# Expert rows of a two-layer decoder step: gated and added by VectorE from loaded rows, or scaled at PSUM eviction and added by accumulating transfers

## The reference, cut to what matters

```
prob  = softmax(x @ router_w)                     # choose a group of 4, then its best 2 experts
gate  = prob[two experts] / sum(prob[two experts])
out   = sum over the two: gate * ((silu(x @ w_gate) * (x @ w_up)) @ w_down[e])
x     = layer_norm(ALPHA * x + out) * g + b       # ALPHA = 4 ** 0.25, eps = 1e-5
```

## Time and profile before

| | |
|---|---|
| median of 3 runs | 1471.41 us (1467.73 to 1471.97) |
| profiled execution, from first to last instruction | 1465.0 us |
| TensorE busy | 1253.8 us, 86% |
| VectorE busy | 916.1 us, 63% |
| ScalarE busy | 698.6 us, 48% |
| GpSimd busy | 252.7 us, 17% |

### The profile page before, as it was taken

One profiled execution on the slowest core, in us unless ns is written; L12 is line 12 of the kernel. 1 busy time (PEld: TensorE's weight loads), 2 busy tenths in 40 slices (PEclk: granted clock), 3 DMA queues, 4 the chain that ended last, 5 costly groups with the idle time before them and its releaser, 6 DMA issues.

```text
span 1465.0 us, 16900 instructions
## 1 busy us (share of the span) xinstructions
PE 1253.8 (86%) x5888; PEld 963.9 (66%) x5888; DVE 916.1 (63%) x1112; ACT 698.6 (48%) x748; POOL 252.7 (17%) x261
## 2 busy tenths in 40 slices
PE   5989994599999996299999999989937999999930
PEld 4766764478888885277776666657736788888820
DVE  4256357498888885832321444464675988888836
ACT  4233223277777775222112544432224777777721
POOL 2021020241111121410000000000302411112314
PEclk9999995699999998599999999969858999999975
DMA  9302047269999996732230133213462899999842
GB/s 341 122 29 93 1 173 285 84 224 359 374 372 372 376 368 214 296 116 92 89 116 1 59 116 115 78 48 118 187 238 83 302 376 373 369 375 371 299 181 77
DMA packets 142529, 302.56 MB, mean 207 GB/s; under 512 B 11888, under 2 KB 12048, under 8 KB 142352
## 3 DMA queue, kind: packets, MB, share of 16 engines
q1 hardware_dynamic: 123024, 250.23, 47.9%
q0 software_dynamic: 19168, 51.31, 9.8%
q10 hardware_dynamic: 288, 0.36, 0.1%
HBM read 288.36 MB, written 30.28 MB: 217 GB/s over the span
## 4 chain that ended last, share of the span: by engine, by line
PE 78%; DVE 13%; DMA 3%; ACT 3%; issue 2%; POOLq 0%; POOL 0%; SPq 0%; DVEq 0%; ACTq 0%
PE ps L1422 20%; PE ps L1424 20%; PE ps L1423 20%; PE ps L1657 3%; DVE wl L868 2%; PE ps L1720 2%; PE ps L1705 2%; PE ps L1581 2%; DVE x L1225 2%; PE ps L1467 2%; ACT wh L617 2%; PE ps L1674 1%; PE ps L1691 1%; DMA xg<-x_rows,gcur 1%; DMA yl<-y_rows 1%
## 5 line engine op out<-in xcount | busy, mean ns | idle before, releaser
L868 DVE TENSOR_TENSOR wl<-raw,wh 128x2048 fp32r<-128x2048 f32 x210 | 481.0, 2314 | 221.3 <-ACT wh L617 217.4
L617 ACT ACTIVATE wh<-raw 128x2048 fp32r<-128x2048 f32 x210 | 398.4, 1915 | 202.0 <-PE ps L1424 138.0
L1422 PE MATMUL ps<-wh,xTh 128*128 128x512 f32 (+1 forms) x560 | 227.7, 407 | 22.8 <-DVE wl L868 14.8
L1424 PE MATMUL ps<-wh,xTl 128*128 128x512 f32 (+1 forms) x560 | 223.0, 398 | 0.0
L1423 PE MATMUL ps<-wl,xTh 128*128 128x512 f32 (+1 forms) x560 | 223.0, 398 | 0.0
L1422 PE MATMUL ps<-wh,xgTh 128*128 128x512 f32 x512 | 209.3, 409 | 6.7 <-DVE xgTl L1175 5.7
L1423 PE MATMUL ps<-wl,xgTh 128*128 128x512 f32 x512 | 203.9, 398 | 0.0
L1424 PE MATMUL ps<-wh,xgTl 128*128 128x512 f32 x512 | 203.5, 398 | 0.0
L1422 PEld LDWEIGHTS ps<-wh,xTh 128*128 128x128 f32 (+1 forms) x560 | 98.6, 176 | 58.9 <-issue 22.5
L1422 PEld LDWEIGHTS ps<-wh,xgTh 128*128 128x128 f32 x512 | 97.3, 190 | 36.2 <-DVE wl L868 8.3
L1424 PEld LDWEIGHTS ps<-wh,xTl 128*128 128x128 f32 (+1 forms) x560 | 98.0, 175 | 34.2
(11 more groups left out here) (258 smaller groups left out, 1641.1 us busy)
## 6 DMA issues: line engine op xcount, KB each, us to landing
raw<-in_moe_w_up SPq DMA_DIRECT2D x120, 1024.0 KB, 10.5
raw<-in_moe_w_down SPq DMA_DIRECT2D x62, 1024.0 KB, 11.7
raw<-in_a_w_in SPq DMA_DIRECT2D x8, 1024.0 KB, 16.7
ahead_up<-in_moe_w_up SPq DMA_DIRECT2D x8, 1024.0 KB, 8.7
yl<-y_rows POOLq DMA_DIRECT2D x8, 1024.0 KB, 8.4
raw<-in_cache_k SPq DMA_DIRECT2D x16, 512.0 KB, 3.8
raw<-in_cache_v SPq DMA_DIRECT2D x16, 512.0 KB, 4.9
raw<-in_a_w_out SPq DMA_DIRECT2D x4, 1024.0 KB, 5.1
```

The lines of the kernel that those rows point to most:

```text
L617: act.activation(wh[:, slot], src, ACT.Copy).then_inc(high[key], 1)
L868: dve.tensor_tensor(wl[:, slot], src, wh[:, slot].bitcast(F32), ALU.subtract).then_inc(low[key], 1)
L1422: pe.matmul(out, high_, w_high, start=start, stop=False)
L1424: return pe.matmul(out, low_, w_high, start=False, stop=stop)
```

## The change

`y_out_` now evicts with a scale for each row: `gslot[:, i]`, the gate of the token in that row divided by ALPHA. `gslot` is built like the index lists: VectorE makes `hi32` (block one-hots times gate / ALPHA), ScalarE widens `lo16` to `lo32`, TensorE multiplies them in ten float32 matmuls, VectorE copies the result from PSUM (`gate_columns`). The rows of `y_rows` are so already gated. Ten accumulating transfers add them to x in SBUF: five with the first choices, then five with the second, each of which GpSimd issues after the first one on the same tile has landed. The sum is x + out / ALPHA instead of ALPHA * x + out; the layer norm divides that factor out again, with eps / ALPHA^2. The multiplies by ALPHA on GpSimd, the buffer `yl` and VectorE's two multiply-adds for each tile are gone. Some semaphores are merged, which moves nothing.

```diff
@@ SyncE
-                    sp.wait_ge(y_in[4], 16)
+                    sp.wait_ge(y_in[4], 32)
@@ GpSimd, moe_pool
-                scale(range(0, 2))
                 gather(3)
-                scale(range(2, 3))
                 scatter(0)
-                scale(range(3, TILES))
...
-                pairs = y_rows[l].rearrange("(k n) d -> n k d", k=2)
-                for t in range(TILES):
-                    pool.dma_start(yl[0:ROWS[t], t], dram_tile(t, pairs)).then_inc(y_in[t], 16)
+                for k in range(2):
+                    for t in range(TILES):
+                        if k:
+                            pool.wait_ge(y_in[t], 32 * l + 16)
+                        pool.dma_start(x[0:ROWS[t], t], dram_tile(t, y_rows[l][k * NTOK:(k + 1) * NTOK]),
+                                       accum_op=ALU.add).then_inc(y_in[t], 16)
                 gain(2 + 2 * l, x)
@@ ScalarE, y_out_ and before the first xg_high
-                    act.activation(yb[:], ps[:, 4:6].rearrange("p a n -> p (a n)"), ACT.Copy).then_inc(s["y_ready"], 1)
+                    act.wait_ge(gate_list, l + 1)
+                    act.activation(yb[:], ps[:, 4:6].rearrange("p a n -> p (a n)"), ACT.Copy,
+                                   scale=gslot[:, bass.ds(i, 1)]).then_inc(s["y_ready"], 1)
...
+                act.wait_ge(onehots, l + 1)
+                act.activation(lo32[:], lo16[:], ACT.Copy).then_inc(slots32, 1)
@@ VectorE, end of route, before xg_low(0), add_experts
-                link(dve.tensor_tensor(gates[:], gates[:], col[:, 6, 1].unsqueeze(1).broadcast_to([P, 2, TILES]),
-                                       ALU.mult))
+                link(dve.scalar_tensor_tensor(out=gates[:], in0=gates[:], scalar=1.0 / ALPHA,
+                                              in1=col[:, 6, 1].unsqueeze(1).broadcast_to([P, 2, TILES]),
+                                              op0=ALU.mult, op1=ALU.mult))
+                link(dve.tensor_tensor(hi32[:], iota[:, 0:LIST_COLS].unsqueeze(1).broadcast_to(hi_shape),
+                                       block_of.broadcast_to(hi_shape), ALU.is_equal))
+                dve.tensor_tensor(hi32[:], hi32[:],
+                                  gates[:].rearrange("p k t -> p (k t)").unsqueeze(2).broadcast_to(hi_shape), ALU.mult
+                                  ).then_inc(gates_at, 1)
...
+            def gate_columns(l):
+                dve.wait_ge(gate_sums, l + 1)
+                dve.tensor_copy(gslot[:], ps[:, 7, 0:LIST_COLS]).then_inc(gate_list, 1)
...
                 def produce(t):
-                    m = ROWS[t]
-                    dve.wait_ge(s["scaled"], t + 1)
-                    dve.wait_ge(y_in[t], 16 * (l + 1))
-                    for k in range(2):
-                        link(dve.scalar_tensor_tensor(out=x[0:m, t], in0=yl[0:m, t, k], scalar=gates[0:m, k, t:t + 1],
-                                                      in1=x[0:m, t], op0=ALU.mult, op1=ALU.add))
+                    dve.wait_ge(y_in[t], 32 * (l + 1))
@@ TensorE, before turn_x(0)
+                pe.wait_ge(slots32, l + 1)
+                pe.wait_ge(gates_at, l + 1)
+                for n in range(2 * TILES):
+                    mm = pe.matmul(ps[:, 7, 0:LIST_COLS], lo32[:, n], hi32[:, n], start=(n == 0),
+                                   stop=(n == 2 * TILES - 1))
+                mm.then_inc(gate_sums, 1)
                 turn_x(0)
```

More of the change, by code:

```diff
@@ L214, in trunk @@
         hb, n = place("hb", [P, HALF], F32, n)
+        lo32, _ = place("lo32", [P, 2 * TILES, P], F32, n)
         hTh, n = place("hTh", [P, 4, P], F32R, n)
@@ L217, in trunk @@
         yb, n = place("yb", [P, D], F32, n)
-        yl, _ = place("yl", [P, TILES, 2, D], F32, arena)
         lg, n = place("lg", [P, TILES, EXPERTS], F32, n)
@@ L234, in trunk @@
         hi16, n = place("hi16", [P, 2 * TILES, LIST_COLS + 1], F16, n)
+        hi32, n = place("hi32", [P, 2 * TILES, LIST_COLS], F32, n)
+        gslot, n = place("gslot", [P, LIST_COLS], F32, n)
         ahead_up = [place(f"ahead_up{q}", [P, 4, HALF], F32, xT_at + q * slot_bytes)[0] for q in range(4)]
@@ L249, in trunk @@
         pages_in = sem("pages_in")
-        x0_high = sem("x0_high"); x0_low = sem("x0_low")
-        rw_high = sem("rw_high"); rw_low = sem("rw_low")
+        inputs_high = sem("inputs_high"); inputs_low = sem("inputs_low")
         wsm_zeroed = sem("wsm_zeroed"); ws_masked = sem("ws_masked")
@@ L282, in trunk @@
         logit_max = sem("logit_max"); plan = sem("plan"); onehots = sem("onehots"); masks = sem("masks")
+        slots32 = sem("slots32"); gates_at = sem("gates_at"); gate_sums = sem("gate_sums"); gate_list = sem("gate_list")
         moe = [{k: sem(f"{k}{l}") for k in (
             "gcopy", "gathered", "xg_tr", "xg_high", "xg_low", "silu", "h_ready", "h_tr", "h_high", "h_low",
-            "y_ready", "scopy", "scattered", "xg_zero", "scaled")} for l in range(LAYERS)]
+            "y_ready", "scopy", "scattered", "xg_zero")} for l in range(LAYERS)]
         ident = con[:, C_IDENT:C_IDENT + P]
@@ L528, in scatter @@
                                             bounds_check=2 * NTOK - 1, oob_is_err=False).then_inc(s["scattered"], 16)
-                def scale(tiles):
-                    for t in tiles:
-                        m = ROWS[t]
-                        pool.tensor_scalar(x[0:m, t], x[0:m, t], ALPHA, None, ALU.mult).then_inc(s["scaled"], 1)
                 gather(0)
@@ L660, in _ @@
                 act.wait_ge(xT0_in[half], 32)
-                act.activation(xTh[:, 4 * half:4 * half + 4], xT0[:, 4 * half:4 * half + 4], ACT.Copy).then_inc(x0_high, 1)
+                act.activation(xTh[:, 4 * half:4 * half + 4], xT0[:, 4 * half:4 * half + 4], ACT.Copy).then_inc(inputs_high, 1)
                 split_a(half)
             act.wait_ge(rw_in, 16)
-            act.activation(rwh, rw_raw[:], ACT.Copy).then_inc(rw_high, 1)
+            act.activation(rwh, rw_raw[:], ACT.Copy).then_inc(inputs_high, 1)
             for j in range(4):
@@ L891, in ln_stats @@
                 link(dve.bn_aggr(mv[0:m, t], stats[0:m, t].rearrange("p a b -> p (a b)")))
-                dve.tensor_scalar(lns[0:m, 0, t:t + 1], mv[0:m, t, 1:2], EPS, None, ALU.add).then_inc(ln_var, 1)
+                eps = EPS / ALPHA ** 2 if call in (2, 4) else EPS
+                dve.tensor_scalar(lns[0:m, 0, t:t + 1], mv[0:m, t, 1:2], eps, None, ALU.add).then_inc(ln_var, 1)
             def ln_scale(call, t):
@@ L942, in _ @@
             for half in range(2):
-                dve.wait_ge(x0_high, half + 1)
+                dve.wait_ge(inputs_high, half + 1)
                 w = (slice(None), slice(4 * half, 4 * half + 4))
-                dve.tensor_tensor(xTl[w], xT0[w], xTh[w].bitcast(F32), ALU.subtract).then_inc(x0_low, 1)
+                dve.tensor_tensor(xTl[w], xT0[w], xTh[w].bitcast(F32), ALU.subtract).then_inc(inputs_low, 1)
                 split_a(half)
-            dve.wait_ge(rw_high, 1)
-            dve.tensor_tensor(rwl, rw_raw[:], rwh.bitcast(F32), ALU.subtract).then_inc(rw_low, 1)
-            dve.wait_ge(rw_low, 1)
+            dve.wait_ge(inputs_high, 3)
+            dve.tensor_tensor(rwl, rw_raw[:], rwh.bitcast(F32), ALU.subtract).then_inc(inputs_low, 1)
+            dve.wait_ge(inputs_low, 3)
             dve.wait_ge(gb_in, 16)
@@ L1199, in body @@
                     xg_low(i + 1)
+                gate_columns(l)
                 xg_low(0)
@@ L1216, in add_experts @@
             def add_experts(l):
-                s = moe[l]
                 def produce(t):
-                    m = ROWS[t]
-                    dve.wait_ge(s["scaled"], t + 1)
-                    dve.wait_ge(y_in[t], 16 * (l + 1))
-                    for k in range(2):
-                        link(dve.scalar_tensor_tensor(out=x[0:m, t], in0=yl[0:m, t, k], scalar=gates[0:m, k, t:t + 1],
-                                                      in1=x[0:m, t], op0=ALU.mult, op1=ALU.add))
+                    dve.wait_ge(y_in[t], 32 * (l + 1))
                 return produce
@@ L1436, in project @@
                     if key == "a" and s < 2:
-                        pe.wait_ge(x0_low, s + 1)
+                        pe.wait_ge(inputs_low, s + 1)
                     for t in range(TILES):
@@ L1524, in route @@
             def route(l, m0, t0, call):
-                pe.wait_ge(rw_low, 1)
+                pe.wait_ge(inputs_low, 3)
                 bank = bank_for(m0)
```

## The result

The changed kernel takes 1479.92 us (median of 9 runs, 1478.17 to 1489.35); the kernel before took 1471.97 us in the same series (9 runs, 1467.66 to 1475.29). The ratio is 1.0069, with a 95% interval of 1.0047 to 1.0092: slower, by 8 us in the medians and by 10 us by the ratio. The profiled executions differ by 13.1 us, because the one of the kernel before lies some 5 us under its own median.

What follows compares the result with a forecast made beforehand. TensorE was taken to bound most of the 1465.0 us, the change acting only where it stands still. Terms -0.3 - 1.0 + 0.2 - 0.5 = -1.6 us gave 1469.8 us from 1471.4, range 1456 to 1488.

Steps and rivals of the forecast that it cites:

- The half rate: Layer ends: accumulating transfers deliver at rate r = 210 GB/s, half the plain loads' 420; r from 180 to 227, chance 0.35.
- my lags: Layer ends: time from first issue until data flow, 3.1 us in layer 1 and 3.9 in layer 0, from the plain loads.
- free addition: Rival at the layer ends: accumulating costs nothing or nearly so, r from 227 up; at 420, 1455.7 us; chance 0.32.
- a rate under 180: Rival at the layer ends: accumulating transfers become the wait; at 140 GB/s +16.5 us, 1487.9 us; chance 0.33.
- The step that failed at the ends: From the third tile's statistics on, multiply-adds leave the path: 19.47 us become 15.57 in layer 1, 11.92 become 9.28 in layer 0.
- my -0.3: Both layer ends together at 210 GB/s: layer 1 0.8 us earlier, layer 0 0.5 us later, sum -0.3 us.
- -0.5 us: Layer 1's end: GpSimd's fourth gain, 3.35 us beside the multiply-adds, takes as little as 2.35; between 0 and -1.0, taken as -0.5.
- The step that failed in the loop: Expert loop: the scaled eviction's extra 0.09 us is hidden by TensorE, bare only after the last block: +0.2 us for both layers.
- The start of the experts: Ahead of the first block: ten new gate matmuls end about when its rows arrive; between 0 and 0.3 us, taken as 0.
- The multiplies by ALPHA: GpSimd's multiplies vanish, so two weight splits beside them no longer slow and TensorE's 0.53 us loss goes: -1.0 us for both layers.
- SyncE's later loads: Loads behind the last y load start some 8 us later at 210 GB/s; no cost up to about 30 us of delay.
- a later end of the layer: Rival at both layer ends: VectorE waits for the third tile, price 2 x 3.80 MB / r, r below 180; chance 0.33.

Runs made afterwards that it cites:

- the run with the short gain: Changed kernel with GpSimd's multiply by the gain in the two norms behind the experts done on 8 of 1024 columns: 1468.94 us, ratio 0.9980.
- the one with the early shift: Changed kernel with VectorE's shift ahead of the next tile's statistics in the two norms behind the experts: 1473.69 us, ratio 1.0024.
- the late eviction: Changed kernel with ScalarE evicting the expert rows behind the copy of hT and the split of up chunk 2: 1472.99 us, ratio 1.0006.
- the kernel before with two edits: Kernel before, with expert rows evicted behind the split of up chunk 2 and the shift ahead of the statistics: 1475.12 us, ratio 1.0029.
- the changed kernel with both edits: Changed kernel with expert rows evicted behind the split of up chunk 2 and the shift ahead of the statistics: 1466.12 us, ratio 0.9975.

## Why the prediction was wrong

I forecast -1.6 us and no measurable difference; it was +8 us in the medians and +10 us by the ratio. The 1479.92 us lie inside my range of 1456 to 1488, but by luck: I had made that range from the bounds of the transfers' rate, and the rate came out as I had put it. The sum of my steps against the trace:

**The half rate was right.** The third tile was to be complete 21.2 and 22.0 us after the first issue; where VectorE waited for it (the run with the short gain), it came after 22.1 and 21.9. By my lags that is 3.80 MB / (22.1 - 3.1) = 200 GB/s and 211 GB/s, against 210 forecast. With plain copies the first tile's time behind the lag is half: 10.28 - 3.1 = 7.2 us against 17.16 - 3.1 = 14.1. Both other rivals on r, free addition and a rate under 180, are out. The Trainium skill's measure (Collectives: The Full Stack, The bandwidth ceiling), by whose ratio r would be 218, lies close to these. The Trainium skill's fixed price for each transfer (DMA: Bandwidth & Descriptors, Anatomy of one DMA) did not add up over queued ones: by its 2.0 us + bytes / 436 GB/s the six plain copies up to the first tile's second half, five of 512 KB and one of 128 KB, would have taken some 18 us one after the other (an estimate from that page), and they took 10.28.

**The step that failed at the ends: "So in layer 1 the 1454.44 - 1434.97 = 19.47 us become 15.57", "In layer 0 one pair lies in that stretch: 614.65 - 602.73 = 11.92 become 9.28".** They became 19.01 and, by the first projection matmul at 617.60, 12.50 us. I took the multiply-adds away and left every other duration as it was. But the multiply-adds had kept VectorE so late that the shift (1.61 us, 1.21 alone) fell mostly behind the gain. Without them the shift starts with the gain and waits for it. In layer 1 both pairs of multiply-adds left in full, 5.25 us (I had counted 3.90), but three shifts became 1.6 us longer: 19.47 - 5.25 + 4.84 = 19.06. In layer 0 one pair left and two shifts grew: 11.92 - 2.64 + 3.23 = 12.51. So the two stretches are 3.44 and 3.22 us longer than I had them. The operation on one column, which waits for a gain too, costs 1.1 and 1.0 us ahead of the third tile (23.2 and 23.0 us after the first issue instead of 22.1 and 21.9). With 0.9 us of late arrival in layer 1 this is 9.7 us, and the difference between my -0.3 and the measured +9.3. The run with the short gain and the one with the early shift show that the collision is the cause: the shift falls to 1.22 and 1.23 us, with the transfers as they were.

The rows for it lay open. The earlier trace rows show the gain at 2351 ns alone and up to 3376 beside the multiply-adds, and I used them, for -0.5 us, in the one direction that helped. They say that two operations take each other's time; when one leaves, the next to stand beside the gain pays. The Trainium skill has the rule (SBUF — State Buffer, Who interferes with whom): a VectorE instruction with two SBUF inputs and a GpSimd instruction that reads SBUF lock each other out, and who issues first holds the other up for its whole length. The traces agree: the shift waits out a gain that started 0.19 us ahead of it, a gain that started 0.30 us behind a multiply-add takes 3.17 us, and the statistics, with one input, keep their 0.69.

**The step that failed in the loop: "The scaled eviction costs 0.09 us more for 512 columns; inside the loop TensorE hides it".** The size was right for the eviction itself (1.03 to 1.12 us on 1024 columns), but I left out the wait and the register in front of it, 0.14 us, and TensorE hid nothing: the trace of before has TensorE waiting 0.2 us in every block for the chunk that ScalarE splits behind the eviction. I showed no row for it and did not ask which wait came last inside a block. 0.23 us in 13 periods and two layers is 6.1 us, and the late eviction gives back 7.

**The start of the experts** was to cost between 0 and 0.3 us. In layer 1 the ten matmuls run from 1103.08 for 4.43 us, and the first block's transposes begin right behind them at 1107.34. From GpSimd's copy of the first index column to the transposes it takes 6.16 us instead of 5.53: +0.6. They started where I put them, 1.9 us behind that copy (1.8 forecast), but they come out as 20 records of 0.22 us, two for each matmul, and last longer than my 2.0 to 3.8 us:

```profile
1103.08 4.43 PE L1612 MATMUL ps<-hi,lo 128*128 128x25 f32 x20 [4.86 <-DVE hi L1163]
1107.34 1.95 PE L1588 MATMUL ps<-con,xg 128*128 128x128 f32 x8
```

The first block's transposes thus wait for the gates, which I had named as a sign of being wrong. In layer 0 the same transposes came 2.9 us earlier than before. The first gather's issue took 1.09 us there instead of 2.83, which can be 1.7 us of it; the kernel before with two edits shows 2.82 too, and the changed kernel's variants show 1.09 or 1.10. Why is open; I had not looked at it. Moving the matmuls behind the first block was not tried.

**The multiplies by ALPHA** were worth more than twice what I said. TensorE's 0.5 us waits for VectorE's split are gone. The first full period between evictions was 19.39 us in layer 0 and 19.42 in layer 1, 1.2 us above the other periods of the kernel before, and is 18.40 and 18.41 now, like its neighbours: 2.4 us against 1.0 forecast, of which 2.0 are left once the slower eviction is paid. So the blocks cost 6.1 - 2.0 for these periods, 1.1 more up to the first evictions (the lower clock in layer 1), and 1.0 less in the last periods, which differ by about as much from run to run: 4.2 us net. SyncE's later loads cost nothing, as forecast.

The rival on the other side, a later end of the layer, had the right sign and the wrong cause: not the transfers' rate, but what stood beside GpSimd's gain once the multiply-adds were gone, and what stood ahead of ScalarE's split in the loop. Nor was the clock the same, as I had put it: 0.76 in the first 5 us from the first projection matmul instead of 0.83, and 0.66 instead of 1.00 for 5 us in layer 1's first blocks.

## What to carry to other kernels

When an operation leaves an engine, redo the timeline: what ran beside its neighbours changes, and two operations that passed each other by may now start together and wait for each other. An operation that is 0.1 us longer inside a loop is hidden only if the trace shows that the engine which sets the period never waits there, not if that engine is merely busy. And when a transfer that adds runs at half the rate, try to let it do half of the addition, while an engine that would only wait does the other half: here that was worth 7 us over the changed kernel with both edits.

## What the runs showed of the hardware

A transfer that adds into SBUF delivered about 200 to 210 GB/s with the DMA engines full, against some 420 for a plain load. VectorE and GpSimd took each other's time in whole instructions: the one that started second stood until the first had ended, even where it had one column to do (1.45 us instead of 0.16). With adding scatters in the loop the weights landed later (13.9 us after issue instead of 9.3 for a chunk of the up weights), and the period rose by 1.2 us a block. On ScalarE a semaphore wait that is long satisfied, placed ahead of an instruction, cost about 0.06 us a block.
